# Streaming the features and their rest as one 512-wide product in the two early feed-forwards

## The reference, cut to what matters

```
def rms_norm(x, gain):
    y = xf * lax.rsqrt(jnp.mean(xf * xf, axis=-1, keepdims=True) + RMS_EPS)
    return (y * gain).astype(x.dtype)
...
def swiglu(h, w_in, w_out):
    g, u = _split(h @ w_in, (D_FF, D_FF))
    return (jax.nn.silu(g) * u) @ w_out
...
        x = x + swiglu(rms_norm(x, norm_ffn[i]), ffn_w_in[i], ffn_w_out[i])
```

## Time and profile before

| what | us |
|---|---|
| median of 3 runs | 1661.43 |
| lowest and highest run | 1660.62, 1662.23 |
| span of the profiled execution, first to last instruction | 1659.6 |
| busy: PE, PEld | 1619.1 (98%), 1462.8 (88%) |
| busy: DVE, ACT, POOL | 1096.3 (66%), 891.3 (54%), 421.5 (25%) |
| DMA, mean over the span | 160 GB/s |

### The profile page before, as it was taken

One profiled execution on the slowest core, in us unless ns is written; L12 is line 12 of the kernel. 1 busy time (PEld: TensorE's weight loads), 2 busy tenths in 40 slices (PEclk: granted clock), 3 DMA queues, 4 the chain that ended last, 5 costly groups with the idle time before them and its releaser, 6 DMA issues. The chain is left out here.

```text
span 1659.6 us, 26949 instructions
## 1 busy us (share of the span) xinstructions
PE 1619.1 (98%) x10929; PEld 1462.8 (88%) x10929; DVE 1096.3 (66%) x1546; ACT 891.3 (54%) x1401; POOL 421.5 (25%) x460
## 2 busy tenths in 40 slices
PE   8999999999999999999999999999999999999999
PEld 7767899987887889998889998999888999999997
DVE  6875665645576665655577768777646876867763
ACT  6465554434455555443456746566445684756652
POOL 2500100002341120000147802244204690214430
PEclk9999999999999999999999999999999999999999
DMA  7523376556330236665555444766556444376652
GB/s 278 174 77 101 103 205 194 185 197 213 99 135 27 77 102 172 185 186 193 174 195 164 147 133 147 189 185 190 181 154 220 159 153 130 131 204 187 190 179 76
DMA packets 287067, 265.30 MB, mean 160 GB/s; under 512 B 12256, under 2 KB 247520, under 8 KB 286944
## 3 DMA queue, kind: packets, MB, share of 16 engines
q1 hardware_dynamic: 286944, 263.59, 50.8%
HBM read 262.52 MB, written 1.05 MB: 159 GB/s over the span
## 5 line engine op out<-in xcount | busy, mean ns | idle before, releaser
L144 DVE TENSOR_TENSOR w_lo<-w_raw,w_hi 128x2048 fp32r<-128x2048 f32 (+2 forms) x244 | 565.8, 2321 | 288.6 <-ACT w_hi L143 283.6
L143 ACT ACTIVATE w_hi<-w_raw 128x2048 fp32r<-128x2048 f32 (+2 forms) x244 | 462.9, 1902 | 214.6 <-PE bank L529 125.5
L1873 PE MATMUL bank<-h_hi,w_hi 128*128 128x256 f32 x1984 | 565.5, 285 | 4.7 <-issue 1.2
L1874 PE MATMUL bank<-h_lo,w_hi 128*128 128x256 f32 x1984 | 561.3, 283 | 0.0
L1875 PE MATMUL bank<-h_hi,w_lo 128*128 128x256 f32 x1984 | 561.2, 283 | 0.0
L1873 PEld LDWEIGHTS bank<-h_hi,w_hi 128*128 128x128 f32 x1984 | 380.5, 192 | 8.2 <-issue 7.5
L1874 PEld LDWEIGHTS bank<-h_lo,w_hi 128*128 128x128 f32 x1984 | 380.7, 192 | 0.1
L1875 PEld LDWEIGHTS bank<-h_hi,w_lo 128*128 128x128 f32 x1984 | 380.6, 192 | 0.0
L456 PE MATMUL bank<-w_hi,h_hi 128*128 128x512 f32 (+1 forms) x288 | 113.4, 394 | 5.4 <-DVE w_lo L144 3.3
L2953 POOL TENSOR_TENSOR cffn_hidden<-cffn_conv 128x256 f32<-128x256 f32 x44 | 73.7, 1675 | 155.5 <-ACT cffn_conv L2984 155.5
L457 PE MATMUL bank<-w_lo,h_hi 128*128 128x512 f32 (+1 forms) x288 | 111.9, 388 | 0.0
(11 more groups left out here) (447 smaller groups left out, 2858.0 us busy)
## 6 DMA issues: line engine op xcount, KB each, us to landing
w_raw<-in_w_in SPq DMA_DIRECT2D x48, 1024.0 KB, 5.0
w_raw<-in_ffn_w_in SPq DMA_DIRECT2D x88, 512.0 KB, 5.0
w_raw<-in_w_up SPq DMA_DIRECT2D x88, 512.0 KB, 5.2
w_raw<-in_ffn_w_out SPq DMA_DIRECT2D x22, 1024.0 KB, 4.9
w_raw<-in_w_down SPq DMA_DIRECT2D x22, 1024.0 KB, 5.0
w_raw<-in_nsa_w_in SPq DMA_DIRECT2D x10, 1024.0 KB, 5.2
w_raw<-in_mem_w_kv SPq DMA_DIRECT2D x8, 1024.0 KB, 5.1
w_raw<-in_w_branch SPq DMA_DIRECT2D x8, 1024.0 KB, 5.1
```

The lines of the kernel that those rows point to most:

```text
L143: return act.activation(hi, raw, ACT.Copy)
L144: return dve.tensor_tensor(self.lo[:, cut_slot, 0:k * n], raw, hi.bitcast(F32), ALU.subtract)
L1873: pe.matmul(out, h, hi[:, f, :], start=(f == 0), stop=False)
L1874: pe.matmul(out, h, lo[:, f, :], start=False, stop=False)
```

## The change

In the two early feed-forwards a job now issues two matmuls for each pair of tile and row tile in place of three: weight hi by feature hi and feature lo together, 512 columns wide, which fills a whole bank (hi product in the first half, lo product in the second), and weight lo by feature hi, 256 wide, summed into the second half. A job therefore takes two banks, one for the gate and one for the up part; the pairs (2, 3), (4, 5), (6, 7), (0, 1) are used in turn, and the last job takes (0, 1). `h_hi` and `h_lo` become two halves of one buffer `h`, so that one access pattern (`pair`) spans both.

The two halves of each bank have to be added behind the job. VectorE reads a bank and one operand of SBUF, so ScalarE first copies the second half of each bank to a new buffer `low` (two copies a job, the first as soon as the gate tile is done), and VectorE adds: gate j = first half + low, and, further down in its turn, hidden j = first half + low for the up part. The multiplication by the row factor, which VectorE had done in L1819, goes to GpSimd, in place on `gate`, between VectorE's addition and ScalarE's silu. The product hidden times gate now reads both operands from SBUF. The down part, the other feed-forwards and all weights are as they were. All code below gets other line numbers: L143 and L144 become L149 and L150.

```diff
@@ -45,6 +45,12 @@
 def heads(tensor, col, nh, dh, width):
 
     return free(tensor[:, :, :], [[width, T], [dh, nh], [1, dh]], col)
+
+
+def pair(hi, lo):
+
+    return bass.AP(tensor=hi.tensor, offset=hi.offset,
+                   ap=[list(hi.ap[0]), [lo.offset - hi.offset, 2], [1, hi.shape[-1]]])
 
 
 def row_bcast(dram, n, offset=0):
@@ -922,14 +928,16 @@
     def __init__(self, nc, stack):
         self.nc = nc
         self.stack = stack
-        self.bank = [stack.enter_context(nc.psum_tensor(f"bank{i}", [P, 512], F32)) for i in range(8)]
+        self.banks = stack.enter_context(nc.psum_tensor("bank", [P, 8 * 512], F32))
+        self.bank = [self.banks[:, 512 * i:512 * i + 512] for i in range(8)]
         self.x = self.keep("x_rows", [P, T, D])
         self.ident = self.keep("ident", [P, P])
         self.gains_1 = self.keep("gains_1", [P, 8 * KD + 4])
         self.mix_gain, self.ffn_gain = self.keep("mix_gain", [P, KD]), self.keep("ffn_gain", [P, KD])
         self.half_power = self.keep("half_power", [P, 1])
         self.row_stat = self.keep("row_stat", [P, 5, T])
-        self.h_hi, self.h_lo = self.keep("h_hi", [P, KD, S], F32R), self.keep("h_lo", [P, KD, S], F32R)
+        self.h = self.keep("h", [P, 2, KD, S], F32R)
+        self.h_hi, self.h_lo = self.h[:, 0, :, :], self.h[:, 1, :, :]
         self.tables = self.keep("rope_tables", [P, 2, 4, 8])
         self.raw = self.keep("w_raw", [P, Weights.RAW, Weights.SIZE])
         self.w_hi = self.keep("w_hi", [P, Weights.CUT, Weights.SIZE], F32R)
@@ -1699,7 +1707,6 @@
 def block_memory_ffn(k, a, layer):
 
     nc = k.nc
-    BANKS = (2, 3, 0, 1)
     with ExitStack() as st:
         k.open(st, f"mf{layer}", nsa_first(a) if layer == 0 else branches_first(a, 0), 0)
         s, w = k.sems, k.weights
@@ -1708,6 +1715,7 @@
         wide_hi, wide_lo = k.small("wide_hi", [P, KF, S], F32R), k.small("wide_lo", [P, KF, S], F32R)
         cols = k.gains_1[:, (1 + 4 * layer) * KD:(4 + 4 * layer) * KD]
         gate, hidden = k.small("gate", [P, 2, S]), k.small("hidden", [P, 2, S])
+        low = k.small("low", [P, 2, 2, S])
         k.attention_buffers()
         next_gain = s("next_gain")
         rows_q = Features(k, "rows_q", k.x, cols[:, 0:KD], h_hi, h_lo, k.norm_scratch, 4, first=4)
@@ -1723,6 +1731,13 @@
         down = Residual(k, "down", a["ffn_w_out"][layer], KF, wide_hi, wide_lo, bank=4, final=True, then=after,
                         factor=rows_f.rstd)
         opened, silu, prod, hid_hi, hid_lo = s("opened"), s("silu"), s("prod"), s("hid_hi"), s("hid_lo")
+        half_done, lowered, scaled_gate, summed = s("half_done"), s("lowered"), s("scaled_gate"), s("up_summed")
+
+        def banks(j):
+            return (0, 1) if j == KF - 1 else ((2, 3), (4, 5), (6, 7), (0, 1))[j % 4]
+
+        def free_bank(j):
+            return (prod, KF - 2) if j == KF - 1 else (prod, j - 3) if j >= 4 else (row_factors.done, 1) if j == 2 else None
 
         k.ready()
         with nc.Block() as block:
@@ -1740,6 +1755,11 @@
                 att.pool(pool, 0)
                 att.pool(pool, 1)
                 rows_f.factors(pool, 4)
+                pool.wait_ge(row_factors.done, 1)
+                for j in range(KF):
+                    pool.wait_ge(opened, j + 1)
+                    pool.tensor_tensor(gate[:, j % 2, :], gate[:, j % 2, :], row_factors.rows, ALU.mult)\
+                        .then_inc(scaled_gate, 1)
 
             @block.scalar
             def _(act):
@@ -1766,7 +1786,16 @@
                 row_factors.act(act)
                 for j in range(KF):
                     w.round_to(act, up[j] + 2)
-                    act.wait_ge(opened, j + 1)
+                    if j >= 2:
+                        act.wait_ge(summed, j - 1)
+                    for tile in range(2):
+                        if tile == 0:
+                            act.wait_ge(half_done, j + 1)
+                        else:
+                            act.wait_ge(w.used, up[j] + 1)
+                        act.activation(low[:, j % 2, tile, :], k.bank[banks(j)[tile]][:, S:2 * S], ACT.Copy)\
+                           .then_inc(lowered, 1)
+                    act.wait_ge(scaled_gate, j + 1)
                     act.activation(gate[:, j % 2, :], gate[:, j % 2, :], ACT.Silu).then_inc(silu, 1)
                     if j >= 1:
                         act.wait_ge(prod, j)
@@ -1813,20 +1842,25 @@
                 for j in range(KF + 1):
                     if j < KF:
                         w.cut_to(dve, up[j] + 2)
-                        dve.wait_ge(w.used, up[j] + 1)
-                        if j == 0:
-                            dve.wait_ge(row_factors.done, 1)
-                        dve.tensor_tensor(gate[:, j % 2, :], k.bank[BANKS[j % 4]][:, 0:S], row_factors.rows, ALU.mult)\
+                        dve.wait_ge(lowered, 2 * j + 1)
+                        if j >= 2:
+                            dve.wait_ge(prod, j - 1)
+                        dve.tensor_tensor(gate[:, j % 2, :], k.bank[banks(j)[0]][:, 0:S], low[:, j % 2, 0, :], ALU.add)\
                            .then_inc(opened, 1)
                     if j >= 1:
                         i = j - 1
                         dve.wait_ge(silu, i + 1)
-                        if i >= 2:
-                            dve.wait_ge(hid_lo, i - 1)
-                        dve.tensor_tensor(hidden[:, i % 2, :], k.bank[BANKS[i % 4]][:, S:2 * S], gate[:, i % 2, :], ALU.mult)\
+                        dve.wait_ge(summed, i + 1)
+                        dve.tensor_tensor(hidden[:, i % 2, :], hidden[:, i % 2, :], gate[:, i % 2, :], ALU.mult)\
                            .then_inc(prod, 1)
                     if j >= 2:
                         hid_rest(j - 2)
+                    if j < KF:
+                        dve.wait_ge(lowered, 2 * j + 2)
+                        if j >= 2:
+                            dve.wait_ge(hid_lo, j - 1)
+                        dve.tensor_tensor(hidden[:, j % 2, :], k.bank[banks(j)[1]][:, 0:S], low[:, j % 2, 1, :], ALU.add)\
+                           .then_inc(summed, 1)
                 hid_rest(KF - 1)
                 if layer == 1:
                     dve.wait_ge(next_gain, 16)
@@ -1850,7 +1884,8 @@
 
                 residual.pe(pe, part=part)
                 for j in range(KF):
-                    stationary_job(k, pe, up[j], k.bank[BANKS[j % 4]], rows_f, (prod, j - 3) if j >= 4 else None, j == 0)
+                    split_job(k, pe, up[j], banks(j), rows_f.hi, rows_f.lo, half_done, free_bank(j),
+                              rows_f if j == 0 else None)
                     if j == 0:
                         row_factors.pe(pe)
                 down.pe(pe, lambda pe, f: pe.wait_ge(hid_lo, f + 1))
@@ -1875,6 +1910,28 @@
             ins = pe.matmul(out, l, hi[:, f, :], start=False, stop=(f == KD - 1))
         if tile == 0 and middle is not None:
             middle(pe)
+    ins.then_inc(w.used, 1)
+
+
+def split_job(k, pe, c, banks, hi, lo, half_done, free_bank=None, features=None, middle=None):
+
+    w = k.weights
+    w.wait_cut(pe, c)
+    if free_bank is not None:
+        pe.wait_ge(*free_bank)
+    whi, wlo = w.halves(c)
+    for tile in range(2):
+        bank = k.bank[banks[tile]]
+        for f in range(KD):
+            if tile == 0 and features is not None:
+                features.wait_feature(pe, f)
+            h, l = whi[:, f, tile * P:(tile + 1) * P], wlo[:, f, tile * P:(tile + 1) * P]
+            pe.matmul(bank[:, :], h, pair(hi[:, f, :], lo[:, f, :]), start=(f == 0), stop=False)
+            ins = pe.matmul(bank[:, S:2 * S], l, hi[:, f, :], start=False, stop=(f == KD - 1))
+        if tile == 0:
+            ins.then_inc(half_done, 1)
+            if middle is not None:
+                middle(pe)
     ins.then_inc(w.used, 1)
```

## The result

The changed kernel takes 1691.14 us (median of 4 runs, 1690.01 to 1694.83) against 1661.71 for the kernel before: the ratio is 1.0183, 95% interval 1.0168 to 1.0197. The change costs 29.4 us. The span of the profiled execution is 1689.8. I had forecast 1680.

The account below looks back on a forecast made before the run. TensorE bounds the kernel, but a VectorE and ScalarE cycle lengthened from 5.25 to 6.18 us takes over; 9.3 us a layer, + 18.6 in all, takes 1661.4 to 1680. Range 1668 to 1697; 1675 to 1684 had chance 0.65.

Parts of the forecast that it names:

- The cycle: VectorE and ScalarE wait for each other in the jobs: 5.25 us a turn, 6.18 with the row factor on GpSimd.
- The rival with 6.51: GpSimd (POOL) waits for two VectorE instructions before its multiplication: cycle 6.51 us, time 1693; chance 0.20.
- the link: Row factor multiplication on GpSimd between gate and silu, inside the cycle: 0.82 us longer alone, 0.93 with VectorE's product.
- The copies and additions: ScalarE's two copies and VectorE's additions and product in each job fit into existing waits: cost nothing.
- The sum: Down chunk 2 starts 9.3 us later in each of two layers: + 18.6 us in all, runs 1680.
- the cover before down chunk 2: TensorE's spare time at down chunk 2 in the kernel before: 4.5 us, ready at 333.46, used at 337.97.
- the wait forecast at down chunk 2: TensorE waits for the rest of down chunk 2 and starts on it at about 347.2 in place of 337.97.
- The clock: Rival: TensorE standing still 0.6 us in each 6.2 lowers the granted clock to 1.2 GHz; 1698, chance 0.03.
- The matmuls: Each of 704 triples in the jobs goes from 0.360 to 0.3467 us: 9.4 us less if TensorE sets the pace.
- The first rival: The multiplication on GpSimd costs nothing and TensorE keeps the pace: 1652, chance 0.09, or 1661, chance 0.03.

Follow-up runs that it names:

- The bank order alone: Changed kernel with bank pairs in the order (2, 3), (0, 1), (4, 5), (6, 7), so the last job's pair was read four jobs ago: 1678.69 us.
- the other mended kernels: Changed kernel with ScalarE rounding chunk j + 3 ahead of the silu: 1656.95 us; those adding the new bank order too: 1656.73 us, further edited 1656.84 and 1655.44.
- both mendings: Changed kernel with ScalarE's rounding of chunk j + 3 ahead of the silu and bank pairs (2, 3), (0, 1), (4, 5), (6, 7): 1656.73 us.

## Why the prediction was right, and by how much it was off

*The cycle.* Right: 6.155 for 6.18, the waits of TensorE 0.55 for 0.63, the silu 1.39 behind the gate for 1.38, GpSimd's 0.74 and 0.85, let in after one instruction of VectorE. The rival with 6.51 did not come. That the cycle is closed by program order, and that the link's place in it is what costs, is shown by the kernel with the rounding ahead of the silu.

*The copies and additions.* Right: the cycle without the link is 5.25.

*The sum.* It had a term missing, and so 18.6 came out where 29.4 was measured. The prediction works out when each chunk is ready and lets job 21 start with its own, but never asks for the bank that it writes. That pair was last written by job 19, and the product of job 19 is made in turn 20, at 333.76, a whole turn after job 21's chunk is ready at 327.30. How far this product lags behind TensorE sets the wait. It starts 4.97 us after the start of job 20 in the kernel with the rounding ahead, where job 21 does not wait; 5.57 without the factor (wait 0.43); 11.7 with the factor on VectorE (6.45); 12.5 in the changed kernel (7.12). Part of the wait is hidden by the cover before down chunk 2. About 2.4 us come on top, 8.05 - 5.65, because half of job 21 runs at 1.2 GHz. The bank order alone gives 12.45 us back, 6.2 a layer, and leaves 17.6 of the forecast 18.6. In the changed kernel the wait forecast at down chunk 2 is not there: the chunk was ready when TensorE came, 10.94 us after the start of the down part, which is 48 matmuls of 0.2267 and 0.06.

*The range and luck.* 1691 lies inside the range of 1668 to 1697 but outside the 1675 to 1684 that had a chance of 0.65, and it lies next to the 1693 of a later POOL. By the time alone that rival would look right; it is the gates, 6.155 apart and not 6.51, that rule it out. The range was wide enough because of a longer cycle and a lower clock, and not because a bank wait was thought of: that it held the measured time is in part luck. Two numbers do not follow from the prediction's own working: three fifths of 18.6 are 11.2, which gives a lower end of 1672.6 and not 1668, and a cycle of 6.25 gives 1683 and not 1684.

*The clock.* The rival tied it to standstills of 0.6 us in each job. Waits that cost 0.5 us a job left it at 1.00; one standstill of 7 us in each layer was followed by 0.50.

*The matmuls.* Half right. The forecast pair of 0.3467 stands in layer 0 of the kernel without the factor (jobs 5.55 apart), but in the other mended kernels and in that kernel's layer 1 it is 0.3533, a job of 5.66: 704 x 0.0067 = 4.7 us less than the 9.4 forecast, in line with the 4.4 us that the kernel with both mendings gains. The trace without the factor is of the fastest of its ten executions, 1656.25, so what it shows of layer 0 need not hold for the median of 1657.55. In the changed kernel it did not matter, since TensorE waited.

*The first rival*, a link that costs nothing, fell with the first turn. It is true of the same link in another place of the order.

## What to carry to other kernels

An engine that is busy for half of a stage can set its pace, if its instructions and another engine's form a loop through both program orders. Walk the loop, add up its links, and compare it with the bounding engine's period: here 5.24 against 5.76, and a link of 0.9 us turned a gain of 4 into a loss. Before moving work to an idle engine look whether the link can lie beside the loop; one instruction moved in ScalarE's order was worth 34 us.

When another engine takes over the pace, all waits have to be worked out again with the new one, above all those at a loop's end that break the pattern. A reuse distance of two jobs in place of four cost nothing with the product 5 us behind the start of job 20, and 7 us with it 12.5 behind. Nor does the loop have to set the pace for that: with a turn of 5.71 us and a job of 5.66 TensorE never waited for a chunk in the jobs, but the loop began behind and could not catch up, and the wait was 6.45 us.

## What the hardware showed beyond that

- The moving operand may lie in two pieces 8 KB apart at no measurable cost (1656.73 and 1656.84 us).
- A 512-wide and a 256-wide matmul in turn take 0.3467 us in some stretches and 0.3533 in others of the same execution, where streams of one width gave 0.2267 + 0.120. Eight of a kind in a row take 0.349 a pair. Neither the layout nor the alternation explains all of it, and what decides between the two stays open.
- GpSimd's multiplication waits for a VectorE instruction with two SBUF operands (0.85 for 0.74) and not for one with an operand in PSUM (0.74); VectorE's next instruction with two SBUF inputs then waits for GpSimd (0.85 for 0.42).
- In the standstill of 7 us in front of the last job the granted clock fell to 0.50, and it was back at about 339.4, when the job had run for 5 us; with waits that cost 0.5 us in each job it stayed at 1.00.
